# Feed-forward gate and up by seven block products in place of eight, in two passes over the tokens, with the residual added by rows at the end

## The chip, the cores and the metric

The kernel runs on one core of one Trainium2 chip. The metric is device time in microseconds (us), as the median of several executions. TensorE (PE) multiplies and writes to PSUM, eight banks of 512 fp32 numbers per partition; VectorE (DVE), ScalarE (ACT) and GpSimd (POOL) do the rest; SyncE (SP) issues the DMAs here.

## The reference, cut to what matters

One layer of a streaming encoder for 1024 new frames and 32 frames of a running stream, 1056 tokens in all, with 1024 features each. Two kinds of attention come first; the change leaves them alone. What it touches is the tail:

```python
def residual_tail(h, oa, ob, g_out_a, g_out_b, w_out, g_ffn, w_gate, w_up, w_down):
    mixed = jnp.concatenate([rmsnorm(oa, g_out_a), rmsnorm(ob, g_out_b)], axis=-1)
    h = h + mixed @ w_out
    u = rmsnorm(h, g_ffn)
    return h + (jax.nn.silu(u @ w_gate) * (u @ w_up)) @ w_down      # D_FF = 2816
```

and a last `rmsnorm` over each row. All is fp32.

## The kernel before

**Products of fp32 numbers.** Each operand is split into a high and a low part (`hi` is the value rounded to the type fp32r by an ACT copy, `lo` is the rest, a subtraction on DVE), and `product` issues three matmuls: hi with hi, hi with lo, lo with hi (lines 604, 605 and 606). So each matmul "of 128x384" below is one third of a product.

**Stages.** Input projection and both attentions run to about 567 us of the span. Then a stage that this text calls the row stage works tile by tile (nine tiles of 128 tokens, the last of 32): `turn_mixed` transposes attention outputs, `out_product` multiplies by `w_out` (24 matmuls 512 wide), DVE adds the residual `h` in `xb`/`xc`, normalises it to `xn2`, and `turn_residual` transposes both on PE, `xc` (eight transposes, the residual by columns, kept in `y_res`) and `xn2` (eight more, split into `f_hi` and `f_lo`).

**Feed-forward.** The 2816 hidden features are taken 256 at a time (`q`, eleven steps). `gate_up(q)` makes gate and up of two blocks of 128 features over all tokens, in three chunks of 384, 384 and 288 tokens, 8 blocks of input features each; `down(q-1)` follows it on PE. ACT takes silu of the gate in PSUM, DVE multiplies (L1877), ACT and DVE split the hidden values (L1465, L1880), DVE adds the down products to `y_res` in SBUF (L1891, L1894). Weights come by DMA as 512 KB blocks into three `raw` buffers and are split by ACT (L1092) and DVE (L1522), 128x1024 at a time. GpSimd has no instruction in this stage. Each engine's order is written out by hand, and engines meet by semaphores alone: an instruction that waits holds up everything behind it on its engine.

**End.** `last_down` interleaves the last down products with transposes of finished tiles (`turn_out`), ACT squares and takes the root, DVE scales, SP stores.

Of the kernel before, what the change touches and what calls it, by code (L numbers as in the profile page):

```python
# [377 lines left out]
def build(nc, x_p, x_s, ck_fox, cv_fox, cl_fox, ck_swa, cv_swa, rel_bias, g_attn, w_in, b_forget, sinks,  # L380
# [2037 lines left out]
```

## Time and profile before

| | |
|---|---|
| median of three runs | 1425.41 us (1424.62 to 1426.76) |
| the profiled execution, its span | 1425.3 us |
| TensorE busy | 1389.4 us, 97% of the span |
| VectorE, ScalarE, GpSimd busy | 572.3, 484.7 and 213.8 us |
| chain that ended last | PE 91% of the span |
| feed-forward stage, from its first matmul to the last one's start | 635.1 to about 1414.7 us |
| granted clock in the feed-forward stage | 1.00 in the stretches of 100 us from 700 to 1300 us |

The profile is of one execution, whose span differs from the median by 0.1 us. A matmul's duration there holds the fill and the drain of the array, which overlap with its neighbours; what a matmul costs in a stream is the distance from its start to the next one's start, called its pitch here.

### The profile page before, as it was taken

The numbers are of one execution on the slowest core, as the hardware profiler recorded it, in microseconds if no ns is written. First come the engines' busy times: TensorE is split into PE (matmuls) and PEld (weight loads), VectorE is DVE, ScalarE is ACT, GpSimd is POOL, SyncE is SP. The second block draws the span as 40 slices with busy tenths as digits, with TensorE's granted clock in tenths as the row PEclk, the third lists the DMA queues.
The fourth block names the chain that finished last, engine by engine and source line by source line (L and its number), as shares of the span: only waits on it lengthen the run. The fifth ranks groups of instructions, "written<-read, shape, count | busy, mean of one in ns | idle before, by whom it ended". The sixth has DMA issues, their size and how long they took to land.

```text
span 1425.3 us, 22561 instructions
## 1 busy us (share of the span) xinstructions
PE 1389.4 (97%) x9041; PEld 1288.1 (90%) x9041; DVE 572.3 (40%) x1340; ACT 484.7 (34%) x1049; POOL 213.8 (15%) x318
## 2 busy tenths in 40 slices
PE   7999999999999899999999999999999999999998
PEld 5988898788878677889999999999999999999997
DVE  6345634242323433562333434342424252525156
ACT  6356555655554552563212121212121212121103
POOL 3145551644443230000000000000000000000000
PEclk9999999999999899999999999999999999999999
DMA  7621124212120444314202020202020202020003
GB/s 202 115 67 38 32 78 156 81 43 80 51 83 15 150 163 135 109 46 132 61 30 68 22 74 16 74 16 74 16 74 16 75 16 74 16 74 15 30 1 122
DMA packets 110255, 97.64 MB, mean 69 GB/s; under 512 B 15936, under 2 KB 96928, under 8 KB 109640
## 3 DMA queue, kind: packets, MB, share of 16 engines
q1 hardware_dynamic: 110152, 96.20, 23.0%
q8 instruction: 72, 1.18, 0.4%
q14 instruction: 31, 0.25, 0.1%
HBM read 77.07 MB, written 19.21 MB: 68 GB/s over the span
## 4 chain that ended last, share of the span: by engine, by line
PE 91%; DVE 3%; DMA 2%; ACT 2%; issue 2%; POOL 1%; SPq 0%; ACTq 0%; DVEq 0%
PE ps L604 28%; PE ps L605 26%; PE ps L606 26%; PE ps L808 2%; DMA cb<-c_scratch 1%; PE ps L738 1%; PE ps L956 1%; PE ps L820 1%; PE ps L685 1%; PE ps L897 1%; PE ps L776 1%; DVE ps L1650 1%; DMA ob<-o_scratch 1%; ACT sp_x L1279 0%; PE ps L703 0%
## 5 line engine op out<-in xcount | busy, mean ns | idle before, releaser
L1891 DVE TENSOR_TENSOR outs<-outs,ps 128x384 f32<-128x384 f32 (+1 forms) x264 | 134.5, 509 | 108.3 <-PE ps L606 108.0
L1877 DVE TENSOR_TENSOR gu<-ps,sg 128x384 f32<-128x384 f32 (+1 forms) x66 | 34.6, 524 | 237.8 <-PE ps L606 237.8
L2055 POOL TENSOR_TENSOR pl_x<-sp_x,ph_x 128x512 fp32r<-128x512 f32 (+5 forms) x120 | 102.3, 866 | 170.4 <-ACT sp_x L1279 169.0
L1465 ACT ACTIVATE h_hi<-gu 128x384 fp32r<-128x384 f32 (+1 forms) x66 | 32.9, 498 | 222.4 <-DVE gu L1877 222.4
L1278 ACT ACTIVATE ph_x<-ps,negc 128x512 fp32r<-128x512 f32 (+5 forms) x120 | 63.0, 525 | 84.5 <-PE ps L820 84.5
L1459 ACT ACTIVATE sg<-ps 128x384 f32<-128x384 f32 (+1 forms) x66 | 30.5, 465 | 171.7 <-PE ps L606 171.7
L604 PE MATMUL ps<-f_hi,ff0hi 128*128 128x384 f32 (+1 forms) x264 | 85.7, 325 | 0.0
L604 PE MATMUL ps<-f_hi,ff2hi 128*128 128x384 f32 (+1 forms) x264 | 85.6, 324 | 0.0
L604 PE MATMUL ps<-f_hi,ff3hi 128*128 128x384 f32 (+1 forms) x264 | 85.6, 324 | 0.0
L604 PE MATMUL ps<-f_hi,ff1hi 128*128 128x384 f32 (+1 forms) x264 | 85.6, 324 | 0.0
L605 PE MATMUL ps<-f_lo,ff0hi 128*128 128x384 f32 (+1 forms) x264 | 85.3, 323 | 0.0
L605 PE MATMUL ps<-f_lo,ff1hi 128*128 128x384 f32 (+1 forms) x264 | 85.2, 323 | 0.0
L605 PE MATMUL ps<-f_lo,ff2hi 128*128 128x384 f32 (+1 forms) x264 | 85.2, 323 | 0.0
L605 PE MATMUL ps<-f_lo,ff3hi 128*128 128x384 f32 (+1 forms) x264 | 85.2, 323 | 0.0
L606 PE MATMUL ps<-f_hi,ff0lo 128*128 128x384 f32 (+1 forms) x264 | 85.2, 323 | 0.0
L606 PE MATMUL ps<-f_hi,ff1lo 128*128 128x384 f32 (+1 forms) x264 | 85.1, 322 | 0.0
L606 PE MATMUL ps<-f_hi,ff2lo 128*128 128x384 f32 (+1 forms) x264 | 85.1, 322 | 0.0
L606 PE MATMUL ps<-f_hi,ff3lo 128*128 128x384 f32 (+1 forms) x264 | 85.1, 322 | 0.0
L604 PE MATMUL ps<-h_hi,ff4hi 128*128 128x384 f32 (+1 forms) x240 | 82.2, 342 | 0.6 <-DVE outs L1894 0.5
L604 PE MATMUL ps<-h_hi,ff5hi 128*128 128x384 f32 (+1 forms) x240 | 78.2, 326 | 0.0
L1092 ACT ACTIVATE ff4hi<-raw 128x1024 fp32r<-128x1024 f32 x10 | 10.6, 1060 | 197.0 <-PE ps L606 197.0
L605 PE MATMUL ps<-h_lo,ff5hi 128*128 128x384 f32 (+1 forms) x240 | 77.5, 323 | 0.0
(303 smaller groups left out, 3837.5 us busy)
## 6 DMA issues: line engine op xcount, KB each, us to landing
raw<-in_w_gate SPq DMA_DIRECT2D x22, 512.0 KB, 4.5
raw<-in_w_up SPq DMA_DIRECT2D x22, 512.0 KB, 5.0
raw<-in_w_down SPq DMA_DIRECT2D x22, 512.0 KB, 3.9
raw<-in_w_in SPq DMA_DIRECT2D x14, 512.0 KB, 4.0
cb<-c_scratch SPq DMA_DIRECT2D x4, 1312.0 KB, 7.1
xt<-in_x_prompt SPq DMA_DIRECT2D x8, 512.0 KB, 4.7
out<-outb SPq DMA_DIRECT2D x16, 256.0 KB, 2.8
ob<-o_scratch SPq DMA_DIRECT2D x16, 256.0 KB, 3.1
```

Source lines behind the costliest of these rows:

```text
L604: pe.matmul(out, wh, xh, start=start, stop=False)
L605: pe.matmul(out, wh, xl, start=False, stop=False)
L606: return pe.matmul(out, wl, xh, start=False, stop=stop)
L685: mm = pe.transpose(ps[0:m, b, (2 * kv + x) * P:(2 * kv + x + 1) * P], ot_w[kv][:, x * m:(x + 1) * m], ident[:])
L738: pe.matmul(ps[0:rows, 2 + kv, 0:2 * m].rearrange("p (x q) -> p x q", x=2), keys[hs, k0:k0 + rows], queries[half][hs, :, q], start=(part = ...
L808: pe.matmul(ps[0:rows, b + h, 0:n], keys[i % 2][hs, k0:k0 + rows], queries[i % 2][hs, q], start=(part == 0), stop=False)
L1278: act.activation(ph_x[2 * (v % 2) + h][0:rows, 0:n], ps[0:rows, b + h, 0:n], ACT.Exp, bias=decay, scale=-1.0)
L1459: act.activation(sg[c][:, 0:n], bank(c, n), ACT.Silu).then_inc(S["g_sg"], 1)
L1465: act.activation(h_hi[par][:, f, c0:c0 + n], gu[(f + c) % 2][:, 0:n], ACT.Copy).then_inc(S["g_hi"], 1)
L1877: dve.tensor_tensor(gu[(f + c) % 2][:, 0:n], bank(3 + c, n), sg[c][:, 0:n], ALU.mult)\
L1891: add = dve.tensor_tensor(y, y, bank(b, whole * P).rearrange("p (t m) -> p t m", t=whole), ALU.add)
L2055: pool.tensor_tensor(pl_x[at][0:rows, 0:n], sp_x[at][0:rows, 0:n], ph_x[at][0:rows, 0:n].bitcast(F32), ALU.subtract).then_inc(S["x_pl"], 1)
```

## The change

Gate and up together multiply a 2x2 block matrix of weights (gate or up, by the first or the last four blocks of input features) by a 2x2 block matrix of inputs (input features by token half). The new code forms four sums of weight blocks and four of input blocks, makes seven products of blocks 4 x 128 features deep in place of eight, and adds them up: `x1` and `p7` are copied out of PSUM by ACT, five are added by DVE (`add_bank`, L2033), one (`p7`) is added again by GpSimd (`add_fourth`, L2373).

- The tokens are taken in two passes: tokens 0 to 511 in halves of 256, and tokens 512 to 1055 in halves of 272. All weights are loaded and split once in each pass. A set `g` is one block of 128 hidden features in one pass; there are 44 sets (`SETS`), 22 (`NF`) in each pass.
- A set has seven `ffn_product`s of 12 matmuls, 256 or 272 wide, on six PSUM banks; seven weight blocks of 128x512, each split by ACT (L1543) and DVE (L2007) into one of eleven slots; four weight sums on GpSimd (`weight_sums`, 128x512, into the single buffer `sums`). From set 2 on it has four down pieces: 24 matmuls 512 wide in the first pass, 48 of 272 in the second (`down_piece`), added to `y` by DVE (L2073), and one down weight of 128x1024 split (`down_hi`, `down_lo`).
- The seven inputs `fu` have one buffer, so pass 1's are made at sets 20 to 22 (`input_sum` on GpSimd, `input_hi` on ACT, `input_lo` on DVE, 128x1088).
- The residual is no longer transposed. It is stored to DRAM (`x2_scratch`) in the row stage and loaded at the end into `hrow`; `add_row` adds the transposed `y` to it. The rows of pass 0 are finished within sets 24 and 25.

The core of the diff:

```diff
-            def residual_columns(t):
-                columns_lo(t, (6, 7), "c_hi3", 2 * t, f_hi, f_lo, t * P, "c_lo3")
...
+            for g in range(SETS):
+                for i in range(7):
+                    ffn_product(g, i)
+                    if g == 0 and i == 2:
+                        turn_residual(TILES - 1)
+                    if g == NF + 2:
+                        if i < 4:
+                            turn_out(i)
...
+                    elif g >= 2 and 2 <= i < 6:
+                        down_piece(g, i - 2)
...
             def turn_residual(t):
-                pe.wait_ge(S["c_h2"], 2 * (t + 1))
...
-                rows_to_columns(t, xc[t % 2], (4, 5), S["c_t2"])
                 pe.wait_ge(S["c_xn2"], t + 1)
...
+            def add_bank(g, i):
+
+                n, par = HALF_OF[pass_of(g)], g % 2
+                first, x2, x3 = x1[:, 0:n], x23[par][:, 0, 0:n], x23[par][:, 1, 0:n]
+                gate0, gate1 = sg[par][:, 0, 0:n], sg[par][:, 1, 0:n]
+                dst, src = {1: (gate0, first), 2: (x2, first), 4: (x3, x2), 5: (gate1, x3), 6: (x2, x2)}[i]
...
+            def down_group(n, q, j):
...
+                pe.wait_ge(S["f_hl"], 4 * pg + 4)
+                pe.wait_ge(S["dw_lo"], n - 1)
...
+            def weight_sums(g):
+
+                a11, a12, a21 = (fraw[g % 2][:, mat, k:k + 4, :] for mat, k in (A11, A12, (1, 0)))
+                a22 = fraw[g % 2][:, 1, 4:8, :]
+                s1, s2, s3, s4 = (sums[:, SUM_OF[i], :, :] for i in (4, 2, 3, 5))
+                pool.wait_ge(S[f"fw_in{g % 2}"], 32 * (g // 2 + 1))
+                if g >= 1:
+                    pool.wait_ge(S["fw_lo"], 7 * (g - 1) + 5)
+                pool.tensor_tensor(s1, a21, a22, ALU.add).then_inc(S["fw_sum"], 1)
+                pool.wait_ge(S["fw_sum"], 4 * g + 1)
+                pool.tensor_tensor(s2, s1, a11, ALU.subtract).then_inc(S["fw_sum"], 1)
+                pool.tensor_tensor(s3, a11, a21, ALU.subtract).then_inc(S["fw_sum"], 1)
...
+                pool.tensor_tensor(s4, a12, s2, ALU.subtract).then_inc(S["fw_sum"], 1)
...
+            def store_mixed(t):
+
+                m = rows_of(t)
+                sp_.wait_ge(S["c_h2"], 2 * t + 2)
+                sp_.dma_start(x2_dram[t * P:t * P + m, :], xc[t % 2][0:m]).then_inc(S[f"x2_out{t % 2}"], 16)
```

**Where the instructions go on DVE.** Before, in the middle of a feed-forward step, VectorE alternates between gated values (`gu`), their low parts (`h_lo`) and weight splits 128x1024 (`ff0lo` and so on), then adds sixteen down products (`outs`):

```order
L1877 TENSOR_TENSOR gu_190<-ps,sg_189 128x288 [waits g_lo,g_sg,g_mm]
L1880 TENSOR_TENSOR h_lo_125<-gu_190,h_hi_124 128x288 [waits g_hi]
L1522 TENSOR_TENSOR ff0lo<-raw_60,ff0hi 128x1024 [waits cw_hi]
L1522 TENSOR_TENSOR ff1lo<-raw_61,ff1hi 128x1024 [waits cw_hi]
L1522 TENSOR_TENSOR ff2lo<-raw_62,ff2hi 128x1024 [waits cw_hi]
L1877 TENSOR_TENSOR gu_191<-ps,sg_187 128x384 [waits g_lo,g_sg,g_mm]
L1880 TENSOR_TENSOR h_lo_125<-gu_191,h_hi_124 128x384 [waits g_hi]
L1877 TENSOR_TENSOR gu_190<-ps,sg_188 128x384 [waits g_lo,g_sg,g_mm]
L1880 TENSOR_TENSOR h_lo_125<-gu_190,h_hi_124 128x384 [waits g_hi]
L1877 TENSOR_TENSOR gu_191<-ps,sg_189 128x288 [waits g_lo,g_sg,g_mm]
L1880 TENSOR_TENSOR h_lo_125<-gu_191,h_hi_124 128x288 [waits g_hi]
L1891 TENSOR_TENSOR outs<-outs,ps 128x3x128 [waits d_y,d_mm] x16
```

After, these are the first twelve of the nineteen rows of one set in pass 0 on VectorE (`fw` are the weight slots, `sums` and `fraw` what they are split from, `x_0`, `x_1`, `x_199` partial sums, `f_p7`, `f_sg`, `f_add` count GpSimd's, ScalarE's and its own work):

```order
L2033 TENSOR_TENSOR x_1_222<-x_1_222,ps 128x256 [waits f_p7,f_pe]
L2043 TENSOR_TENSOR sg_216<-sg_216,x_1_222 128x256 [waits f_add,f_sg]
L2007 TENSOR_TENSOR fw_196<-sums,fw_196 128x512 [waits fw_hi]
L2007 TENSOR_TENSOR fw_197<-sums,fw_197 128x512 [waits fw_hi]
L2050 TENSOR_TENSOR h_lo_174<-sg_216,h_hi_173 128x256 [waits f_hh]
L2033 TENSOR_TENSOR sg_220<-x_199,ps 128x256 [waits f_x,f_pe]
L2007 TENSOR_TENSOR fw_198<-sums,fw_198 128x512 [waits fw_hi]
L2033 TENSOR_TENSOR x_0_190<-x_199,ps 128x256 [waits f_x,f_pe]
L2073 TENSOR_TENSOR y<-y,ps 128x512 [waits y_add,d_pe]
L2007 TENSOR_TENSOR fw_187<-fraw_175,fw_187 128x512 [waits fw_hi]
L2007 TENSOR_TENSOR fw_188<-fraw_176,fw_188 128x512 [waits fw_hi]
L2073 TENSOR_TENSOR y<-y,ps 128x512 [waits y_add,d_pe]
```

The adds of products now stand among the weight splits, and between the gated value (second row) and its low part (fifth row) stand two splits that wait for ScalarE.

**On ACT.** Over the same stretch ScalarE's row is now (`h_hi` high parts of hidden values, `x_199` a product copied out, `sg` silu):

```order
L1592 ACTIVATE h_hi_214<-sg_220 128x256 [waits f_gu] x2
L1577 ACTIVATE x_199<-ps 128x256 [waits f_add,f_pe]
L1543 ACTIVATE fw_197<-sums 128x512 [waits f_pe,fw_sum]
L1543 ACTIVATE fw_198<-sums 128x512 [waits f_pe,fw_sum]
L1584 ACTIVATE sg_216<-sg_216 128x256 [waits f_add]
L1543 ACTIVATE fw_187<-sums 128x512 [waits f_pe,fw_sum]
```

Silu, and with it the split behind it, now waits for an add on VectorE (`f_add`), and the splits ahead wait behind `h_hi`, which waits for VectorE's gated value (`f_gu`).

**On POOL.** Before, GpSimd's last compute rows are those of the attention:

```order
L2055 TENSOR_TENSOR pl_x_106<-sp_x_161,ph_x_103 32x32 [waits x_e]
L2055 TENSOR_TENSOR pl_x_107<-sp_x_162,ph_x_155 32x32 [waits x_e]
```

After, it has six rows for each set:

```order
L2340 TENSOR_TENSOR sums<-fraw_176 128x512 [waits fw_lo,fw_in0]
L2342 TENSOR_TENSOR sums<-sums,fraw_176 128x512 [waits fw_sum]
L2343 TENSOR_TENSOR sums<-fraw_176 128x512
L2347 TENSOR_TENSOR sums<-fraw_176,sums 128x512 [waits fw_lo,fw_sum]
L2373 TENSOR_TENSOR x_0_190<-x_0_190,p_179 128x256 [waits f_add,f_x] x2
```

All of them are new there, and the first starts when VectorE has finished the second of the two splits after its gated value.

## Rows read from the trace of the kernel before

**Rows 1.** Page, part 1: busy us, share of the span, instructions.

```profile
PE 1389.4 (97%) x9041; PEld 1288.1 (90%) x9041; DVE 572.3 (40%) x1340; ACT 484.7 (34%) x1049; POOL 213.8 (15%) x318
```

**Rows 2.** Windows: stretch, length, busy PE, PEld, DVE, ACT, POOL, clock, DMA share, GB/s.

```profile
800.00:900.00 100.00, 100.00 (x613) 99.15 (x612) 43.34 (x87) 15.48 (x23) 0.00 (x0) 1.00 0.14 41
```

**Rows 3.** Timeline of PE (start us, duration us): streams 384, 288, 256 and 512 wide.

```profile
159.13 0.28 PE L604 MATMUL ps<-ph_w,vs_hi 128*128 128x256 f32 x1
...
159.72 0.28 PE L606 MATMUL ps<-ph_w,vs_lo 128*128 128x256 f32 x1
...
568.75 0.39 PE L604 MATMUL ps<-wo_hi,m_hi 128*128 128x512 f32 x1
...
572.19 0.39 PE L604 MATMUL ps<-wo_hi,m_hi 128*128 128x512 f32 x1
...
899.92 0.34 PE L604 MATMUL ps<-f_hi,ff0hi 128*128 128x384 f32 x1
...
902.03 0.29 PE L604 MATMUL ps<-f_hi,ff0hi 128*128 128x288 f32 x1
...
905.22 0.34 PE L604 MATMUL ps<-f_hi,ff1hi 128*128 128x384 f32 x1
```

**Rows 4.** Timeline of PE: both sets of transposes of tile 7, first feed-forward matmul.

```profile
633.46 1.03 PE L956 MATMUL ps<-ident,xb 128*128 128x128 f32 x8
634.33 1.04 PE L956 MATMUL ps<-ident,raw 128*128 128x128 f32 x8
635.13 0.42 PE L604 MATMUL ps<-f_hi,ff0hi 128*128 128x384 f32 x1
```

**Rows 5.** Groups by form, DVE: count, busy us and mean ns, idle before.

```profile
L1891 DVE TENSOR_TENSOR outs<-outs,ps 128x256 f32<-128x256 f32 x88 | 37.0, 421 | 26.1 <-PE ps L606 25.7
...
L1522 DVE TENSOR_TENSOR ff0lo<-raw,ff0hi 128x1024 fp32r<-128x1024 f32 x12 | 14.7, 1225 | 5.1 <-ACT ff0hi L1092 4.9
...
L1528 DVE TENSOR_TENSOR f_lo<-ps,f_hi 128x512 fp32r<-128x512 f32 x16 | 10.3, 685 | 0.0
```

**Rows 6.** Groups by form, ACT.

```profile
L1263 ACT ACTIVATE ot_w<-ps 128x256 f32<-128x256 f32 x32 | 11.7, 384 | 5.0 <-PE ps L606 5.0
...
L1225 ACT ACTIVATE vw_hi<-outb 128x512 fp32r<-128x512 f32 x8 | 5.1, 632 | 0.3
```

**Rows 7.** Groups by form, POOL.

```profile
L2055 POOL TENSOR_TENSOR pl_x<-sp_x,ph_x 128x512 fp32r<-128x512 f32 x48 | 60.8, 1287 | 61.2 <-ACT sp_x L1279 61.2
L2004 POOL TENSOR_TENSOR pl_w<-sp_w,ph_w 128x256 fp32r<-128x256 f32 x60 | 43.0, 738 | 41.4 <-ACT sp_w L1248 41.3
```

**Rows 8.** Timeline, DVE and POOL, in the first stage.

```profile
16.03 1.28 DVE L1734 SCALAR_TENSOR_TENSOR xn<-xt,small,gains 128x1024 f32<-128x1024 f32 x1
...
17.80 2.41 POOL L1989 TENSOR_TENSOR cw0lo<-raw,cw0hi 128x1024 fp32r<-128x1024 f32 x1 [9.47 <-ACT cw0hi L1092]
...
19.31 1.98 DVE L1734 SCALAR_TENSOR_TENSOR xn<-xt,small,gains 128x1024 f32<-128x1024 f32 x1
```

**Rows 9.** Timeline: two pairs back to back, and a handover from DVE to ACT.

```profile
583.14 1.07 ACT L1413 ACTIVATE outs<-ps 128x512 f32<-128x512 f32 x2
...
913.85 0.56 DVE L1877 TENSOR_TENSOR gu<-ps,sg 128x384 f32<-128x384 f32 x1 [2.45 <-PE ps L606]
...
914.44 0.52 ACT L1465 ACTIVATE h_hi<-gu 128x384 fp32r<-128x384 f32 x1 [3.63 <-DVE gu L1877]
...
941.25 0.46 DVE L1880 TENSOR_TENSOR h_lo<-gu,h_hi 128x288 fp32r<-128x288 f32 x1 [0.51 <-ACT h_hi L1465]
941.62 0.55 DVE L1891 TENSOR_TENSOR outs<-outs,ps 128x384 f32<-128x384 f32 x1
```

**Rows 10.** Timeline of the end: transposes after the last matmul, last store issued.

```profile
1414.69 3.65 PE L1061 MATMUL ps<-ident,outs 128*128 128x128 f32 x32
...
1422.89 0.33 SPq L2362 DMA_DIRECT2D out<-raw  x1
```

**Rows 11.** Page, part 6: DMA issues, KB each, median us from issue to landing.

```profile
raw<-in_w_up SPq DMA_DIRECT2D x22, 512.0 KB, 5.0
```

More of the change, by code:

```diff
@@ new lines, in build @@
+        hrow = (*hrows, *hrows, hrow8)
+        early, end = lay(end, *((f"fw{k}", [P, 2, 4, P], F32R) for k in range(3)))
+        (x23_0,), end = lay(end, ("x23_0", [P, 2, 272], F32))
+        assert end <= reg1 + 8 * D * 4
+        late, end = lay(reg1 + 8 * D * 4, *((f"fw{k}", [P, 2, 4, P], F32R) for k in range(3, SLOTS)))
+        fw = (*early, *late)
+        (x1,), end = lay(end, ("x1", [P, 272], F32))
+        assert end <= reg2
+        u_parts, end = lay(reg2, *((f"fu{k}{n}", [P, 4, 272], F32R) for k in range(7) for n in ("hi", "lo")))
@@ L514, in build @@
+        (x23_1,), end = lay(1184 + P * 4, ("x23_1", [P, 2, 272], F32))
+        h_hi, h_lo, sg, x23 = (h_hi0, h_hi1), (h_lo0, h_lo1), (sg_0, sg_1), (x23_0, x23_1)
         ss_col = small[:, 72:72 + 18]
@@ L1082, in _ @@
+            for k, x in enumerate(GROUPS[LAST0:]):
+                down_group(*x)
+                if k == 10:
+                    turn_out(4)
+                if k == 13:
+                    turn_out(5)
+            for t in range(6, TILES):
                 turn_out(t)
@@ new lines, in copy_out, with silu @@
+            def copy_out(g, x):
+                n = HALF_OF[pass_of(g)]
+                i = 3 * x
+                act.wait_ge(S["f_pe"], 7 * g + i + 1)
+                if g >= 1:
+                    act.wait_ge(*((S["f_add"], 5 * (g - 1) + 2) if x == 0 else (S["f_p7"], 2 * (g - 1) + 2)))
+                act.activation((x1, p7)[x][:, 0:n], bank((7 * g + i) % SPARE, n), ACT.Copy).then_inc(S["f_x"], 1)
+            def silu(g, j):
+                n = HALF_OF[pass_of(g)]
+                act.wait_ge(S["f_add"], 5 * g + (1, 4)[j])
+                part = sg[g % 2][:, j, 0:n]
+                act.activation(part, part, ACT.Silu).then_inc(S["f_sg"], 1)
@@ new lines, in _ @@
+            add_bank(SETS - 1, 6)
+            gated(SETS - 1, 0)
+            hidden_lo(SETS - 1, 0)
+            down_lo(SETS + 1)
+            for k, x in enumerate(GROUPS[LAST0:]):
+                add_group(*x)
+                if k == 12:
+                    add_row(4)
+                if k == 14:
+                    add_row(5)
+            for t in (4, 5):
+                out_roots(t, t + 1)
+                out_row(t)
+            for t in range(6, TILES):
+                add_row(t)
@@ L1951, in _ @@
+            for t in range(6, TILES):
+                out_roots(t, t + 1)
+                out_row(t)
         @block.gpsimd
@@ new lines, in add_fourth @@
+            def add_fourth(g):
+                n, par = HALF_OF[pass_of(g)], g % 2
+                for x in range(2):
+                    pool.wait_ge(S["f_x"], 2 * g + 2)
+                    pool.wait_ge(S["f_add"], 5 * g + 3 + x)
+                    part = x23[par][:, x, 0:n]
+                    pool.tensor_tensor(part, part, p7[:, 0:n], ALU.add).then_inc(S["f_p7"], 1)
+            pool.wait_ge(S["g_pe"], NT)
+            pool.wait_ge(S["ev_act"], ALL_ACT)
+            pool.wait_ge(S["ev_dve"], ALL_DVE)
@@ L2365, in _ @@
+            sp_.wait_ge(S["fw_sum"], 4 * (SETS - 1))
+            sp_.wait_ge(S["fw_lo"], 7 * (SETS - 1))
+            load_result_row(8)
+            for t in range(4, TILES):
+                store_result(t)
             sp_.wait_ge(S["st_y0"], 16 * 3)
```

779 lines of the change are left out of this document (479 added, 300 removed).

## The prediction

> **What bounds the kernel now.** I read the page first: TensorE is busy 97% of the span [rows 1]. Then the windows: in the feed-forward stage PE is busy all the time at clock 1.00, while DVE has 43 us of work in 100, ACT 15, POOL none [rows 2]. So that stage lasts as long as its stream of matmuls, and the price of one is its pitch. Twelve starts 384 wide go from 899.92 to 902.03, 0.1755 us each; 24 of 288 from there to 905.22, 0.1329. Five of 256 take 0.59 us, 0.118 each, and 15 of 512 take 3.44 us, 0.2293 [rows 3]. For 272 I take 0.1255, between 256 and 288.
>
> **What PE saves.** Before: gate and up are 22 x 2 x 8 x 3 = 1056 matmuls for each chunk, down 528, and 1584 x (2 x 0.1755 + 0.1329) = 766 us. After: 22 x 84 = 1848 matmuls of 256 (218.1) and as many of 272 (231.9); down 528 of 512 (121.1) and 1056 of 272 (132.5), in all 704 us. That is 62 less. The residual's transposes go too: 0.87 us a tile, the start distance of the two blocks of eight [rows 4], 7.0 for the eight tiles before the first feed-forward matmul.
>
> The Trainium skill (TensorE: Matmul & The Clock Gate, Back-to-back issue gap) gives N/2.4 + 2.5 ns; by it the sum would be 709 us before and 652 after, 57 less. The trace's pitches are 8% longer, and I go by them.
>
> Per set PE then needs 84 x 0.118 + 24 x 0.2293 = 15.4 us in pass 0 and 132 x 0.1255 = 16.6 in pass 1. The question is whether the other engines keep this pace.
>
> **What a set costs DVE, ACT and POOL.** Durations: DVE 0.42 for 256, 0.69 for 512, 1.22 for 1024 [rows 5]; ACT 0.38 for 256 from PSUM, 0.63 for 512 from SBUF, and 0.42 (estimate between these) for 256 from SBUF [rows 6]; POOL 1.29 for 512, 0.74 for 256 [rows 7]. Independent neighbours on DVE start 0.09 before the end (941.25 + 0.46, next at 941.62); two ACT copies of 0.584 take 1.07 together, so 0.10 there; a handover between engines takes 0.03 [rows 9]. DVE's nineteen instructions of a set in pass 0 (7 splits and 4 down adds of 512, one split of 1024, nothing else above 256: 5 adds, 2 gated, 2 low parts) come to 11 x 0.60 + 1.13 + 9 x 0.33 = 10.7 us: below 15.4. But two things stand between them.
>
> First, **exchanges with ACT**: DVE's first splits wait for ACT's, which stand behind `h_hi` and so behind DVE's own gated value; later splits stand behind silu, which waits for DVE's add.
>
> Second, **the port to SBUF**: one DVE instruction with both inputs in SBUF, normally 1.28 us, took 1.98 when a POOL tensor_tensor was running at its start. POOL ended at 20.21, DVE 1.08 later, about the time to stream 1024 elements [rows 8]. So it stood still until POOL was done; for 512 elements I take half, 0.54 after POOL's end, for 1024 1.08. POOL is new in this stage, and all splits, gated values and low parts on DVE have both inputs in SBUF.
>
> The Trainium skill (SBUF — State Buffer, Who interferes with whom) says this: such a DVE instruction and a GpSimd one that reads SBUF exclude each other, and whoever starts first holds the shared port for its whole instruction. The trace agrees.
>
> **A walk through one set**, t = 0 at its first row on DVE, with PE ahead. Add 0 to 0.42; gated 0.45 to 0.87. ACT: `h_hi` 0.90 to 1.32, copy out 1.22 to 1.60, two splits to 2.13 and 2.66. DVE: two splits 2.16 to 2.85 and 2.76 to 3.45, low part to 3.78, add to 4.11. ACT: silu 4.14 to 4.56, split 4.46 to 5.09. DVE split 5.12 to 5.81. POOL's first sum starts when the low part frees the port, 3.78 to 5.07; the second waits for that split, 5.81 to 7.10. DVE: add and down add to 6.74; next split held by POOL, ends 7.64. Third sum to 8.93, split ends 9.47, fourth sum to 10.76; down add to 10.07; the split of 1024, held, ends at 10.76 + 1.08 = 11.84. From there add, split, down add, add: 1.86, to 13.70. Silu 13.73 to 14.15, ACT split to 14.68, DVE split 14.71 to 15.40, gated to 15.73, `h_hi` 15.76 to 16.18, low part to 16.63; the next set starts at 16.54. The sum: 10.7 of work, 3.3 waiting for ACT, 2.5 for the port.
>
> This loop does not contain PE. Two things can only lengthen it: at 5.1 split and second sum ask together (the other outcome adds about 0.5), and POOL may keep the port through queued sums (then 18.0). I take 16.9 for pass 0. Pass 1 has eight down adds at 0.35 for four at 0.60 and nine instructions 0.02 longer: + 0.55, 17.45. Both are above PE's 15.4 and 16.6; PE then waits, for a hidden low part before a down piece (`f_hl`) or for a bank. Were the sums on POOL free of the port, the loop would be 14.1, hidden under PE.
>
> **Edges.** (a) Row stage: DVE has input splits of 128x1024 from tile 6 on, seven of 1.2, for the `f_lo` of 1.3 a tile that go: + 3. The residual's store and the reload behind it have two tiles' time. First product at 635.1 - 7.0 + 3 = 631. (b) Sets 0 and 1: DVE first finishes the last tile (7.6), then splits twelve weights in set 0, with ACT's and POOL's share 16, then 14.5 for set 1, which lacks 2.4 of down adds: 38, where PE needs 20. (c) Sets 20 to 22: 51 + seven input splits 8.4 + four sums of 2.5 on POOL, of which about 6 falls on DVE: 66. (d) Sets 23 to 25: 52 + four row adds of 1.2 and four row scalings of 1.2, and 3 for PE's transposes in turn: 65. (e) Sets 42 and 43 split almost nothing more: PE's 16.6. (f) End: 2 for the last low part, 16 groups of six matmuls (0.75) with two `turn_out`s and the row adds between, 15, then row adds, squares, scalings for five tiles. Before, 10.6 us lay from the last matmul to the end [rows 10]; the new end adds row adds (1.2 each) ahead of the squares: 14. In all 31.
>
> Weight traffic doubles, from 66 blocks of 512 KB (22 of each matrix) to 132, three per set; against the 5.0 us from issue to landing [rows 11] a set of over 15 us leaves it hidden.
>
> **Sum**: 631 + 38 + 18 x 16.9 (304) + 66 + 65 + 16 x 17.45 (279) + 33 + 31 = 1447. The profiled execution of before took 1425.3 and the median 1425.4, so 1447 stands against both. Rounded, as the terms allow no more: **1445 us**, 1.4% slower.
>
> **Rivals.**
> 1. *PE sets the pace* (0.30), the other side. Mechanism: DVE and POOL share the port at less cost, or ACT runs far enough ahead that its exchanges vanish. For it: DVE's work alone is 10.7 of 15.4. Against it: the 1.98 us of rows 8. Time: 629 + 33 + 18 x 15.4 + 56 + 55 + 18 x 16.6 + 29 = 1378; with half the edges' stalls not recovered, 1390. It decides from 0.5 us less per set on: a loop under 16.4 and 16.95 gives below 1425.
> 2. *POOL keeps the port through its four sums* (0.12): 18.0 and 18.55 per set, 34 x 1.1 = 37 more, 1482.
> 3. *Transfers come late* (0.06): two raw buffers, one for down weights, and a gate load that stands behind a down load on SP. If three blocks together took over 8 us, each us more delays POOL's sums by one: + 1 on 34 sets, 1479.
>
> The forecast itself has 0.52, with 1428 to 1472 as its own range. Cases of both signs hold much of the chance: the range goes from rival 1, 1388, to between forecast and rival 2, 1474. Bounds of the unknown cost of the port: nothing (14.1, PE's pace, 1390) and POOL first throughout (1482). A measurement of this kernel tells some 0.2% (3 us) from no change. Faster 0.32 (rival 1, little of the forecast), within it 0.05, slower 0.63.
>
> **What would show it.** In the profile after: matmul pitches 0.118, 0.125 and 0.23, PE work 62 us less; PE idle 1 to 2 us per set, put down to DVE; DVE splits 128x512 with a mean well over 0.69 (about 0.9), single ones up to 1.9, while adds from PSUM stay at 0.42; sets 16.5 to 17.5 us apart. I would be wrong if the splits kept 0.69 next to POOL, if PE is busy throughout sets 3 to 19 (rival 1), or if the splits wait over 3 us at once (rival 2).

## The result, and the profile after

Median of 4 runs after the change: **1473.88 us** (1471.06 to 1477.22); before, in the same series, 1426.09 (1424.62 to 1427.72). Ratio 1.0339, 95% interval 1.0321 to 1.0358: the change makes the kernel 3.4% slower. The forecast was 1445, 1.4% slower: the direction is right, the size is not (48 us more than before, forecast 20). The measured time lies at the upper end of the stated range of 1388 to 1474, and beyond the forecast's own 1428 to 1472. The profiled execution has a span of 1471.1 us.

The page of the kernel after, part 1 (for [rows 1]) and, of part 5, the new groups of VectorE and GpSimd (busy us, mean ns, idle before):

```profile
PE 1354.3 (92%) x9497; PEld 1220.8 (83%) x9497; DVE 914.1 (62%) x1804; ACT 674.9 (46%) x1462; POOL 586.3 (40%) x590
...
L2007 DVE TENSOR_TENSOR fw<-sums,fw 128x512 fp32r<-128x512 f32 x176 | 163.2, 949 | 139.5 <-ACT fw L1543 139.5
...
L2007 DVE TENSOR_TENSOR fw<-fraw,fw 128x512 fp32r<-128x512 f32 x132 | 140.5, 1083 | 12.1 <-ACT fw L1543 11.9
...
L2343 POOL TENSOR_TENSOR sums<-fraw 128x512 f32<-128x512 f32 x44 | 77.8, 1769 | 0.0
```

A split of 512 that took 0.69 us in [rows 5] now takes 0.95 or 1.08 in the mean, a sum of 1.29 on GpSimd [rows 7] takes 1.77, and VectorE waits 139.5 us for ScalarE's high parts.

The same kernel's windows (columns as in [rows 2]): sets 0 and 1; the steady part of pass 0; sets 20 to 22; sets 23 to 25; the rest of pass 1:

```profile
631.00:684.00 53.00, 36.92 (x256) 34.64 (x254) 41.60 (x56) 25.88 (x53) 29.22 (x20) 0.84 0.30 83
684.00:993.00 309.00, 289.42 (x1943) 267.15 (x1942) 241.28 (x379) 126.53 (x252) 144.70 (x110) 0.97 0.34 93
993.00:1062.00 69.00, 54.31 (x332) 49.53 (x331) 53.87 (x71) 28.57 (x50) 30.38 (x19) 0.88 0.33 99
1062.00:1133.00 71.00, 58.02 (x407) 55.92 (x406) 51.24 (x82) 27.93 (x53) 26.92 (x21) 0.90 0.24 68
1133.00:1417.00 284.00, 272.44 (x2118) 267.99 (x2117) 221.36 (x401) 113.38 (x224) 122.89 (x92) 1.00 0.35 101
```

Before, TensorE was busy in all of the stretch of [rows 2]. Now it idles about 1 us a set in the steady parts (1.1 in pass 0, 0.7 in pass 1) and much more at the start and at the change of passes.

**One set, seen on VectorE and GpSimd** (timeline of both engines in the kernel after; start us, us):

```profile
744.43 1.35 POOL L2340 TENSOR_TENSOR sums<-fraw 128x512 f32<-128x512 f32 x1 [5.66 <-DMA fraw<-in_w_up]
...
745.86 1.29 POOL L2342 TENSOR_TENSOR sums<-sums,fraw 128x512 f32<-128x512 f32 x1
745.96 1.75 DVE L2007 TENSOR_TENSOR fw<-sums,fw 128x512 fp32r<-128x512 f32 x1 [1.00 <-ACT fw L1543]
747.09 1.79 POOL L2343 TENSOR_TENSOR sums<-fraw 128x512 f32<-128x512 f32 x1
...
747.62 0.41 DVE L2033 TENSOR_TENSOR x<-x,ps 128x256 f32<-128x256 f32 x1
...
748.55 0.88 DVE L2007 TENSOR_TENSOR fw<-fraw,fw 128x512 fp32r<-128x512 f32 x1
748.83 1.76 POOL L2347 TENSOR_TENSOR sums<-fraw,sums 128x512 f32<-128x512 f32 x1
750.06 1.08 DVE L2007 TENSOR_TENSOR fw<-fraw,fw 128x512 fp32r<-128x512 f32 x1 [0.64 <-ACT fw L1543]
```

GpSimd's second sum ends at 747.15; the split that asked at 745.96 ends at 747.71, 0.56 later. The third sum ends at 748.88, the next split at 749.43, 0.55 later; the fourth at 750.59, the split at 751.14, 0.55 later. The prediction had 0.54. And the third and fourth sums start before the split ahead of them has ended and last 1.8 where 1.29 is usual: GpSimd is held by VectorE in its turn. The add of 0.41, with one input in PSUM, runs in the middle of the third sum at its usual length [rows 5].

**The sum against the trace.** VectorE's split of a down block (L2058) stands once in each set. The first and last start in four stretches of the kernel after (one line's instructions: count, ns min, median and max, first and last start):

```profile
L2058 DVE TENSOR_TENSOR dw<-draw,dw x19: 1206/1212/1726, 683.7 to 992.6; 128x1024 fp32r<-128x1024 f32 x19
...
L2058 DVE TENSOR_TENSOR dw<-draw,dw x4: 1210/1468/1724, 992.6 to 1061.7; 128x1024 fp32r<-128x1024 f32 x4
...
L2058 DVE TENSOR_TENSOR dw<-draw,dw x4: 1209/1220/1724, 1061.7 to 1133.2; 128x1024 fp32r<-128x1024 f32 x4
...
L2058 DVE TENSOR_TENSOR dw<-draw,dw x17: 1210/1211/1626, 1133.2 to 1416.6; 128x1024 fp32r<-128x1024 f32 x17
```

In the prediction's walk this split begins 10 us into a set, so its terms read 679 for the mark of set 2 (631 + 38 + 10) and 54 from the mark of set 42 to the end (33 + 31 - 10). In the table, each run's marks are read in the same way (the expectations of e8 and e16 give 74.6 and 66.2 us for stretches between other marks; here these are 69.1 and 71.5). e1, e3, e4, e7, e8, e15 and e16 are the experiments below; "PE only" is rival 1 (629 + 33 + 10, 18 x 15.4, 56, 55, 16 x 16.6, 52).

| us | forecast | PE only | after | e1 | e3 | e4 | e7 | e8 | e16 | e15 |
|---|---|---|---|---|---|---|---|---|---|---|
| mark of set 2 | 679 | 672 | 683.7 | 674.1 | 674.7 | 678.6 | 671.1 | 683.3 | 683.8 | 680.2 |
| sets 2 to 19 | 304 | 277 | 308.9 | 286.3 | 286.2 | 280.2 | 280.0 | 305.9 | 305.1 | 280.4 |
| sets 20 to 22 | 66 | 56 | 69.1 | 64.0 | 63.7 | 65.4 | 61.4 | 54.8 | 68.7 | 62.7 |
| sets 23 to 25 | 65 | 55 | 71.5 | 66.2 | 66.4 | 63.3 | 62.8 | 71.5 | 65.7 | 63.3 |
| sets 26 to 41 | 279 | 266 | 283.4 | 267.3 | 267.5 | 268.1 | 265.8 | 283.5 | 283.2 | 265.6 |
| to the end | 54 | 52 | 54.5 | 56.0 | 55.9 | 55.9 | 54.5 | 54.5 | 53.4 | 54.6 |
| span | 1447 | 1378 | 1471.1 | 1413.9 | 1414.4 | 1411.5 | 1395.5 | 1453.5 | 1459.8 | 1406.6 |

### The profile page after: what moved, and what is told of

It is laid out like the page before. It is cut to its first block, busy times and chain, and to the rows that moved or that the text cites. A ratio compares the mean times of both kernels' runs of the same rounds, so it can differ in the third digit from the quotient of the medians.

```text
span 1471.1 us, 26068 instructions
## 1 busy us (share of the span) xinstructions
PE 1354.3 (92%) x9497; PEld 1220.8 (83%) x9497; DVE 914.1 (62%) x1804; ACT 674.9 (46%) x1462; POOL 586.3 (40%) x590
## 4 chain that ended last, share of the span: by engine, by line
PE 49%; DVE 23%; issue 13%; ACT 8%; DMA 4%; SPq 1%; POOL 1%; DVEq 0%; ACTq 0%; POOLq 0%
PE ps L702 14%; PE ps L704 13%; PE ps L703 13%; DVE fw L2007 6%; ACT fw L1543 4%; DVE y L2073 3%; PE ps L906 2%; DVE x L2033 2%; DVE sg L2043 2%; DVE h_lo L2050 2%; DVE dw L2058 2%; DVE sg L2033 2%; DMA fraw<-in_w_up 1%; PE ps L836 1%; DMA cb<-c_scratch 1%
## 5 line engine op out<-in xcount | busy, mean ns | idle before, releaser
L2007 DVE TENSOR_TENSOR fw<-sums,fw 128x512 fp32r<-128x512 f32 x176 | 163.2, 949 | 139.5 <-ACT fw L1543 139.5
L702 PE MATMUL ps<-h_hi,dw 128*128 128x272 f32 (+1 forms) x528 | 181.1, 343 | 64.3 <-DVE h_lo L2050 45.5
L2340 POOL TENSOR_TENSOR sums<-fraw 128x512 f32<-128x512 f32 x44 | 62.8, 1426 | 295.7 <-DVE fw L2007 208.8
L704 PE MATMUL ps<-h_hi,dw 128*128 128x272 f32 (+1 forms) x528 | 175.9, 333 | 0.0
L703 PE MATMUL ps<-h_lo,dw 128*128 128x272 f32 (+1 forms) x528 | 175.0, 331 | 0.0
L702 PEld LDWEIGHTS ps<-h_hi,dw 128*128 128x128 f32 x528 | 102.1, 193 | 77.5 <-DVE h_lo L2050 48.4
L2007 DVE TENSOR_TENSOR fw<-fraw,fw 128x512 fp32r<-128x512 f32 x132 | 140.5, 1083 | 12.1 <-ACT fw L1543 11.9
L2373 POOL TENSOR_TENSOR x<-x,p 128x256 f32<-128x256 f32 (+1 forms) x88 | 79.7, 908 | 171.1 <-DVE x L2033 134.9
L1543 ACT ACTIVATE fw<-fraw 128x512 fp32r<-128x512 f32 x132 | 82.3, 627 | 122.2 <-PE ps L704 117.5
L2073 DVE TENSOR_TENSOR y<-y,ps 128x272 f32<-128x272 f32 (+1 forms) x240 | 117.4, 511 | 10.7 <-PE ps L704 10.6
L704 PEld LDWEIGHTS ps<-h_hi,dw 128*128 128x128 f32 x528 | 102.2, 194 | 8.2
L703 PEld LDWEIGHTS ps<-h_lo,dw 128*128 128x128 f32 x528 | 102.9, 195 | 4.3
L1543 ACT ACTIVATE fw<-sums 128x512 fp32r<-128x512 f32 x176 | 104.3, 618 | 1.1 <-PE ps L704 0.9
L2343 POOL TENSOR_TENSOR sums<-fraw 128x512 f32<-128x512 f32 x44 | 77.8, 1769 | 0.0
```

The costliest lines, as they stand in the source:

```text
L702: pe.matmul(out, wh, xh, start=start, stop=False)
L703: pe.matmul(out, wh, xl, start=False, stop=False)
L704: return pe.matmul(out, wl, xh, start=False, stop=stop)
L1543: act.activation(fw[e % SLOTS][:, 0, :, :], weight_block(g, i), ACT.Copy).then_inc(S["fw_hi"], 1)
L2007: dve.tensor_tensor(lo, weight_block(g, i), hi.bitcast(F32), ALU.subtract).then_inc(S["fw_lo"], 1)
L2073: dve.tensor_tensor(dst, dst, bank(6 + at % 2, width), ALU.add).then_inc(S["y_add"], 1)
```

## The experiments

Except for e14 and e15 each time is that of one execution, and executions of one kernel lie up to 6 us apart (1471.06 to 1477.22 above). Beside these single executions the kernel before took 1423.8 to 1426.0. The stretches of the table say more than the totals: e14 is the same kernel as e4, and its trace reads 680.0, 280.1, 65.3, 63.3, 268.0 and 54.5, so the four in the middle repeat within 0.1 and the first and last within 1.4. Where TensorE has pauses, sets 2 to 19 repeat less well, within 3 to 4 (308.9 in the kernel after, 305.1 in e16, whose edit does not touch them).

### The port: e1, e2, e3

e1; e2 has `0:2, 0:128` in place of `0:1, 0:32`, and the other three sums are cut likewise:

```
-                return sums[:, SUM_OF[i], :, :]
+                return fraw[g % 2][:, i % 2, 0:4, :]
...
-                pool.tensor_tensor(s1, a21, a22, ALU.add).then_inc(S["fw_sum"], 1)
+                pool.tensor_tensor(s1[:, 0:1, 0:32], a21[:, 0:1, 0:32], a22[:, 0:1, 0:32], ALU.add).then_inc(S["fw_sum"], 1)
```

> GpSimd's four sums of a set write 32 of 512 columns; the splits of the summed weights read the raw gate and up blocks instead, at the same places and with the same semaphores (this leaves out Strassen's weight sums). GpSimd then reads SBUF for about 0.1 us four times a set in place of 1.3 to 1.8. Theory A (the loop of VectorE, ScalarE and GpSimd sets the pace; port and exchanges add up): without the port's 2.5 us the loop falls to about 14.1 to 14.5, TensorE takes over at 15.4 and 16.6, splits 128x512 return to 0.69, 1410 to 1425 us. Rival B (the exchanges with ScalarE alone, the port costs nothing): sets stay at 17.0 and 17.8, 1465 to 1471. Rival C (TensorE or its clock sets the pace): no change, 1471.

Measured: 1415.87 us.

> As the run with 32 columns, but the four sums write 256 of 512 columns (about 0.7 us each). Theory A: the port costs about half, the loop is about 15.5, near TensorE's pace, so nearly all of the gain is there already: 1415 to 1435. Rival B: 1465 to 1471. If the loss is proportional to GpSimd's time and the loop is bound throughout: half way between the run with 32 columns and 1471.

Measured: 1423.0 us.

e3, with the first of those two edits and, for each of the four sums:

```
-                pool.tensor_tensor(s1, a21, a22, ALU.add).then_inc(S["fw_sum"], 1)
+                pool.wait_ge(S["fw_sum"], 4 * g + 0)
+                pool.memset(sums[:, 0:3, :, :], 0.0).then_inc(S["fw_sum"], 1)
```

> GpSimd works as long as before (four instructions of about 1.3 us a set, at the same places in its queue and behind the same semaphores), but each is a memset of 1536 columns that reads nothing from SBUF; the splits read the raw blocks (this leaves out the weight sums). Theory A (what costs is the port that both read SBUF through): splits at 0.69 and the time of the run with 32 columns, 1410 to 1425. Rival D (not the port but the length of GpSimd's chain, whose late sums hold the splits): stays near 1471. If a memset holds the port as well: splits above 0.69 as now, and 1460 or more.

Measured: 1416.34 us. e3, groups of 700 to 900 us, the splits and one of the four memsets:

```profile
L2007 DVE TENSOR_TENSOR fw<-fraw,fw 128x512 fp32r<-128x512 f32 x90 | 60.6, 690 | 43.8 <-ACT fw L1543 43.8
...
L2343 POOL MEMSET sums<- 128x1536 f32 x13 | 18.0, 1386 | 0.7
```

and e3's window of 700 to 800:

```profile
700.00:800.00 100.00, 99.13 (x685) 91.53 (x683) 72.99 (x135) 45.40 (x90) 49.38 (x40) 1.00 0.35 96
```

GpSimd is busy 49 us in 100, more than the 45 of the kernel after, and the splits are back at 0.690. So not GpSimd's time nor its place in the chain costs the 57 us, but that its instructions read SBUF while VectorE's read two inputs there. The Trainium skill (SBUF — State Buffer, Who interferes with whom) has this rule too: such a VectorE instruction contends with one of GpSimd that reads SBUF, not with one that only writes it; e3 agrees. Rivals B, C and D of the expectations fall. The waits for ScalarE are still there (43.8 us here, 42.2 in the same 200 us of the kernel after) and cost nothing now. In e2, sums of half the width bring back 50 of the 57 us, and all of what sets 2 to 19 and 26 to 41 have to give (286.2 and 267.5 us, as in e1): the loop need only fall to TensorE's pace, and below it a shorter one gains nothing, which is why the gain is not in proportion.

### The exchanges with ScalarE: e4, e12, e13

e4; e12 is its first moved pair alone, e13 the other two (`silu` for 0 and 1):

```
-                if g >= 1:
-                    hidden_hi(g - 1, 0)
...
                 weights_hi(g, 0)
-                silu(g, 0)
+                if g >= 1:
+                    hidden_hi(g - 1, 0)
                 weights_hi(g, 1)
+                silu(g, 0)
...
-                silu(g, 1)
                 weights_hi(g, 4)
+                silu(g, 1)
```

> Only ScalarE's order changes, the computation is whole: the high parts of the weights stand ahead of the hidden high part and of both silus, so VectorE's splits find them done. Theory A: the 3.3 us of waiting for ScalarE go from the loop (17.0 to about 14), TensorE takes over: sets 15.5 and 16.8, 1400 to 1425. Port alone (rival E, the exchanges are hidden anyway): 1460 to 1471. If the port's share grows because VectorE now meets GpSimd more often: 1430 to 1450.

Measured: 1413.4 us. e4's windows:

```profile
700.00:800.00 100.00, 100.00 (x703) 93.30 (x702) 88.30 (x137) 45.93 (x91) 53.56 (x39) 1.00 0.38 103
...
1200.00:1300.00 100.00, 100.00 (x796) 100.00 (x795) 82.94 (x152) 43.05 (x85) 49.96 (x36) 1.00 0.36 96
```

and its splits of 700 to 900 us:

```profile
L2008 DVE TENSOR_TENSOR fw<-sums,fw 128x512 fp32r<-128x512 f32 x52 | 45.3, 892 | 11.6 <-ACT fw L1543 11.2
L2008 DVE TENSOR_TENSOR fw<-fraw,fw 128x512 fp32r<-128x512 f32 x39 | 42.2, 1088 | 2.9 <-ACT fw L1543 2.7
```

VectorE's waits for ScalarE fall from 42 to 14 us in these 200, the splits stay as long as in the kernel after (0.89 and 1.09), VectorE is busy 88 of 100, and TensorE is busy throughout. The port costs as much as before and nothing waits for it.

> The changed kernel, whole, with one edit of ScalarE's order: the high parts of the two weights that VectorE splits first in a set stand ahead of the hidden high part. In the prediction's walk VectorE waits 1.3 us there (0.87 to 2.16), and 0.3 at the second split; with PE's pace at 15.4 and 16.6 and sets of 17.0 and 17.7, about half of the way: sets of 15.6 to 16.0 and 16.7 to 17.0, 1430 to 1445. If the waits only move to the next exchange: 1460 or more.

Measured: 1434.27 us; steady sets 15.5 in pass 0 and 17.45 in pass 1, the second above its range.

> The other two edits of ScalarE's order alone: the high part of the weight behind each silu stands ahead of it. In the walk VectorE waits 1.0 us at the first silu (4.11 to 5.12) and 1.1 at the second (13.57 to 14.71), 2.1 together: sets of 15.4 to 15.6 and 16.6 to 16.8 in the steady stretches, 1418 to 1432. If these waits are hidden by the port's stalls: 1455 or more.

Measured: 1429.93 us; steady sets 15.8 and 16.8 (e4: 15.5 and 16.8). In pass 0 either edit brings the loop to or near TensorE's pace, in pass 1 only the silus' does; that the two gains are so unequal there was not in the walk, and its reason stays open.

### Both away: e7

The edits of e1 and e4 together.

> Both causes taken away: ScalarE's order as in the run of 1413.4, and GpSimd's sums 32 columns wide with the raw blocks split (leaves out the weight sums). If port and exchanges are two parts of one loop, either alone already brings it under TensorE's pace, and together they give little more, only at the change of passes: 1398 to 1410, sets of 15.4 and 16.6. If the two gains add (58 each), far less: 1355.

Measured: 1397.35 us, just below the range. e7's windows of sets 2 to 19 and 26 to 41:

```profile
671.00:951.00 280.00, 279.08 (x1946) 259.86 (x1946) 217.95 (x379) 126.60 (x252) 62.43 (x109) 1.00 0.38 102
...
1075.00:1341.00 266.00, 266.00 (x2115) 266.00 (x2114) 201.63 (x401) 113.46 (x224) 52.70 (x92) 1.00 0.38 108
```

Gains of 57 (e1) and 60 (e4) do not add; together they are 76, the rest of it mostly at the start and in sets 20 to 22. This is the kernel in which TensorE sets the steady pace, 15.5 and 16.6 us a set, and it takes 1397, not rival 1's 1378: the steady sets match its terms and sets 20 to 25 exceed them by 13.

### Transfers: e5, e6

The three blocks stood behind `load_down_raw`, at NF, NF + 4 and NF + 7:

```
                 load_ffn_raw(k + 2)
+                if k == NF + 1:
+                    sp_.wait_ge(S["u_lo"], 14)
+                    for t in range(4):
+                        sp_.wait_ge(S[f"x2_out{t % 2}"], 16 * (5 - t % 2))
+                        load_result_row(t)
+                if k == NF + 5:
+                    for t in range(4):
+                        store_result(t)
+                if k == NF + 8:
+                    for t in range(4, 8):
+                        load_result_row(t)
                 if k >= 1:
                     load_down_raw(k + 2)
```

> Only SyncE's order changes: the loads of result rows 0 to 3 and 4 to 7 and the stores of rows 0 to 3 stand behind the gate and up loads of the next set in place of ahead of them. In the trace after the change two sets of pass 1 take 22.3 and 22.5 us with their sums waiting for the up block, followed by 14.5 and 14.0. If late transfers matter (rival 3 of the prediction), 8 to 12 us go, 1461; by the loop theory the short sets behind already give most of it back, and 2 to 4 us go: 1467 to 1470.

Measured: 1467.26 us. By the marks sets 23 to 25 fall from 71.5 to 68.0 and sets 26 to 41 from 283.4 to 282.1; the other three stretches ahead of them differ by -1.4, -0.5 and +0.9. So late transfers are worth some 5 us (3.5 + 1.3), by rows queued ahead of a set's gate and up blocks. In the kernel after, two first sums of sets 26 to 40 waited for such an up block, in e5 none did. The weights' own traffic is less well hidden than the prediction had it. Among the first sums of sets 2 to 19 of the kernel after, four of 18 waited for the up block last, as here:

```profile
881.16 1.31 POOL L2340 TENSOR_TENSOR sums<-fraw 128x512 f32<-128x512 f32 x1 [6.23 <-DMA fraw<-in_w_up]
```

but the usual wait, for VectorE's split, is 5.66, so this one, the longest of the four, cost 0.6 us at most. Rival 3's mechanism is there in these sets, but hardly its price.

> The run with ScalarE's order changed (1413.4) and SyncE's order of the run before this one together. With TensorE the bound, a wait of the sums for the up block matters only where it reaches TensorE (about 1.5 us at each of two places): 1408 to 1412. If transfers are what is left between this kernel and TensorE's pace, 1400 or less.

Measured: 1414.67 us, no gain over e4's 1413.4 (a miss): sets 26 to 41 fall from 268.1 to 265.9, but sets 23 to 25 take 0.9 more and set 2's mark comes 3.4 later, in a part that the edit doesn't touch.

### The change of passes and the residual's rows: e8, e16

e8, in which VectorE's low part is cut as ScalarE's high part is, then e16:

```
-                act.activation(fu[i][0][:, :, 0:n], staged(p, *U_FROM[i]), ACT.Copy).then_inc(S["u_hi"], 1)
+                act.activation(fu[i][0][:, :, 240 * p:n], staged(p, *U_FROM[i])[:, :, 240 * p:n], ACT.Copy).then_inc(S["u_hi"], 1)
...
-                b11, b12, b21, b22 = (staged(p, k, j) for k in range(2) for j in range(2))
+                b11, b12, b21, b22 = (staged(p, k, j)[:, :, 240 * p:] for k in range(2) for j in range(2))
```

```
-                dve.tensor_tensor(hrow[t][0:m], hrow[t][0:m], ps[0:m, b:b + 2, :].rearrange("p b n -> p (b n)"), ALU.add)\
+                dve.tensor_tensor(hrow[t][0:m, 0:32], hrow[t][0:m, 0:32], ps[0:m, b, 0:32], ALU.add)\
```

> The changed kernel with the input sums and splits of pass 1 cut to columns 240 to 271 (leaves out the rest of pass 1's operands, TensorE multiplies what pass 0 left there); all else as it is. It prices term (c): VectorE loses seven splits of 1.3 us, GpSimd three of its four sums of 2.5 us. If these hold sets 20 to 22, they fall from 74.6 us to 53 to 57, and the whole to 1450 to 1455; if the passes' change costs by the operands that TensorE must release first, it stays above 65 and the whole above 1462.

Measured: 1455.48 us, at the range's upper end. Sets 20 to 22 fall by 14.3, to 54.8, and the interval ahead of them, in which the first input sum of pass 1 now runs, by 2.7 (19.7 to 17.0). The input work was priced at 14.4 in term (c) (8.4 + 6); it costs 17.0, or a little more, as 32 of 272 columns were left.

> The changed kernel with the nine additions of the residual rows at the end cut to 32 of 1024 columns (leaves out the rest of the residual and of the result); loads, squares, scalings and stores stay. It prices the row adds of terms (d) and (f): 1.1 us less for each of nine, four in the set of pass 1 where TensorE's transposes wait for them in turn, three to four on the path at the end. By the prediction's terms 4 to 5 us less in sets 23 to 25 (66.2 to about 61.5) and 3 to 4 at the end: 1463 to 1467. If they are hidden: 1471 to 1474.

Measured: 1461.93 us, a little below the range. Sets 23 to 25 fall by 5.8, the end by 1.1 (3 to 4 were expected there). Of the rest of the 11.3 us of the spans, 3.8 lie in sets 2 to 19, which this edit does not touch.

### The sums on VectorE: e9, e10

Both take `weight_sums` of sets 2 to 43 from GpSimd and put its four instructions on VectorE: the first behind `down_lo`, the second behind the next `add_bank`, the third behind `add_bank(g, 5)`, the fourth at the set's end. e10 has e4's order of ScalarE as well.

```
                 down_lo(g + 1)
+                weight_sum(g + 2, 0)
                 add_bank(g, 4)
+                weight_sum(g + 2, 1)
```

> The changed kernel, whole, with the weight sums of sets 2 to 43 on VectorE in place of GpSimd (four instructions of 0.69, 0.60 from start to start, so 2.4 us more work a set); GpSimd keeps only the two short sums of 256 or 272 columns. By the loop theory the port's 2.5 us are exchanged for 2.4 us of work in the same loop: sets stay at 16.8 to 17.3 and 17.5 to 18, 1463 to 1475. If the port cost more than the theory says, faster than 1455; if VectorE's work was hidden and only GpSimd's late sums counted, 1420.

Measured: 1480.92 us; steady sets 17.4 and 17.8.

> The same sums on VectorE together with ScalarE's order changed (the run of 1413.4). VectorE has 10.7 + 2.4 = 13.1 us of work a set and waits for neither port nor ScalarE: below TensorE's 15.4, so steady sets as in the run of 1413.4; at the change of passes, where VectorE is the bound, the port's stalls of up to 3.3 us on single splits are gone but 2.4 us a set are added: 1405 to 1416.

Measured: 1429.62 us; steady sets 15.7 and 17.3.

Both miss their ranges on the slow side. The port's 2.5 us a set are gone, and 2.4 us of instructions in VectorE's queue cost as much or more. In e9 most sets of pass 0 take 16.9 as in the kernel after; the mean is raised by three of 18.3 to 20.0, in which the granted clock is 0.83 to 0.91. e10 shows it best, at 1.00: VectorE has 88 us of work in 100 in pass 1, as in e4's pass 0, yet its sets take 17.3 where TensorE needs 16.6. That the sums stand ahead of the adds for which the silus wait is the likely reason; a run with other places was not made.

### Squares and scalings spread: e11

e4 with e5's order (its stores and second loads two sets later still), and `out_squares(t)` and `out_row(t)` of rows 0 to 3 one by one in sets 25 to 27:

```
-                if g == NF + 3:
-                    out_roots(0, 4)
-                    for t in range(4):
-                        out_row(t)
...
+                if g in (NF + 4, NF + 5):
+                    out_row(2 * (g - NF - 4))
```

> ScalarE's order and SyncE's order changed as before, and the four squares, four row scalings of the finished rows 0 to 3 spread one by one over the sets behind, in place of four in a row. In the trace of the run of 1414.7 the sets of the scalings took 19.7 and 19.3 in place of 16.6, with TensorE waiting 3.1 twice for a hidden low part: about 6 us less, 1405 to 1410. If the waits come from something else, 1413.

Measured: 1413.06 us, no difference from e4, where 1405 to 1410 was expected. The stalls move from one set to the next (sets 26 to 41: 267.3 against 268.1) and are not less.

### A version faster than both: e14, e15

e15 is e4 and e5 with GpSimd's input sums 1 to 3 of pass 1 put on VectorE, behind the splits that they wait for:

```
                 if g == NF - 1:
                     input_lo(1, 0)
+                    input_sum(1)
```

> The kernel with ScalarE's order changed, whole, the same file as in the run of 1413.4, timed. By its one look: 0.8% faster than the kernel before, 0.991 to 0.993 of it.

Measured: 1415.04 us in the median of five, ratio to the kernel before 0.9931 (0.9917 to 0.9944).

> ScalarE's order, result rows behind the next set's loads, and the three input sums of pass 1 that lie in the change of passes on VectorE in place of GpSimd. In the trace of the run of 1413.4 these three sums of 2.5 us hold VectorE's splits for 2.3, 2.0 and 2.25 us; on VectorE each costs 1.28: about 2.7 us less, and 1 for the rows: 1409 to 1412, 0.989 to 0.991 of the kernel before.

Measured: 1408.05 us in the median of four, just below its range, ratio 0.9878 (0.9862 to 0.9894), against 1424.79 for the kernel before beside both. With ScalarE's queue in another order alone, the seven products are 0.7% faster than the eight; with e15's two further edits, 1.2%. Both gains are small, but neither interval holds 1.

## Why the prediction was right in direction and wrong in size

- **PE's saving**: right. Without port and exchanges a set takes 15.5 and 16.6 (e7), forecast 15.4 and 16.6, and TensorE is busy 1327.5 us in e7, 61.9 less than before (forecast 62). In the kernel after, the same 9497 matmuls keep it busy 1354.3 us, only 35.1 less, as many run at the lower clock (below).
- **The port**: right. a split of VectorE's that meets a sum ends 0.55 us after it (0.54 forecast), adds from PSUM keep their 0.41, and the memsets of e3 show that it is the reading of SBUF that costs. Rival 2 is refuted by the timeline above: between queued sums a waiting split gets its turn.
- **The loop**: right as a mechanism. e3 and e4 each remove one of its parts, each frees TensorE, and together they gain little more than alone. The walk's 16.9 and 17.45 are 16.99 (sets 3 to 18) and 17.71 (sets 26 to 41). The walk said that without the port the loop would hide under PE; the runs show the same of the exchanges. Port and exchanges were not 2.5 and 3.3 us each to be paid, but a loop 1.5 us above TensorE's pace in pass 0 and 1.1 in pass 1; either one, taken away, pays for both.
- **(a)**: right, the first feed-forward product starts at 631.3.
- **The 24 us between the sum, 1447, and the span** are spread over the terms, by the marks. **(b)** + 4.7. **Sets 2 to 19** + 4.9: 2.8 in the last interval, 19.7 long, as the first input sum of pass 1 already falls on a split in it, which (c) had counted later, and 2.1 in the other seventeen. In these VectorE waited for TensorE three times, 1.6 us in all, after falls of its clock (last section), where the walk said: "This loop does not contain PE." The split that the input sum held:

```profile
976.79 2.54 POOL L2358 TENSOR_TENSOR st_b<-st_b 128x1088 f32<-128x1088 f32 x1
...
976.96 2.93 DVE L2007 TENSOR_TENSOR fw<-sums,fw 128x512 fp32r<-128x512 f32 x1 [1.00 <-ACT fw L1543]
```

- **(c)** + 3.1, or 5.9 with that last interval: its input work is 17.0 in place of 14.4 (e8), its base of 51 is 54.8. **(d)** + 6.5: the row adds cost 5.8 in place of 4.8 (e16), and 3.5 come from rows loaded ahead of a set's gate and up blocks (e5), which rival 3 had at a chance of 0.06 and for another reason, the weights' own traffic. **(e) and (f)** + 0.5. **Sets 26 to 41** + 4.4: 16 x 0.26, the extra 0.55 of pass 1 in the walk is 0.72. Here too VectorE waits for TensorE, 14 times and 4.9 us in all, at the clock's upper level; one of them (timeline of the kernel after):

```profile
1262.33 0.44 DVE L2033 TENSOR_TENSOR sg<-x,ps 128x272 f32<-128x272 f32 x1 [0.30 <-PE ps L704]
```

The step that failed is the sizing of the edges, (b), (c) and (d): each was summed from the instructions that were added, at their own durations, as though at the start and at the change of passes the loop lost nothing beyond them. They and the last interval before set 20 came out 17.1 us too short (4.7 + 3.1 + 6.5 + 2.8) of the 24. All six stretches came out longer, none shorter. e7 shows the same of rival 1: steady terms exact, sets 20 to 25 too short by 13. How much of (b) and of the bases of (c) and (d) is the lower clock (below) and how much waiting was not separated, so the cause of those parts stays open.

The steady sets account for 6.5 us more. There it is "This loop does not contain PE" that does not hold: of VectorE's waits in it, 1.6 and 4.9 us are for TensorE. No run separates what these waits add.

That 1473.88 lies inside the range, by 0.1 us, is luck: the range's upper end was taken from rival 2, in which GpSimd keeps the port, and that is not what happened.

Three slips of the prediction changed nothing of this: its list of VectorE's "nineteen instructions" of a set adds up to 21, and its 10.7 us count all 21; rival 1's "from 0.5 us less per set on" gives 1447 - 34 x 0.5 = 1430, and 1425 needs 0.65; and the range's lower end, 1388, lies above rival 1's own 1378.

## What to carry to other kernels

Work moved to GpSimd is not free for VectorE when both read SBUF: count the rest of GpSimd's instruction for each VectorE instruction with two SBUF inputs that meets it, and let GpSimd keep what reads nothing. When a loop of helper engines is a little above the bound, look first at the order within a queue: here three swaps on ScalarE were worth 60 us and left the port's cost in place, hidden. The errors of many small terms, each estimated by adding instructions, did not cancel here: price the transitions (first sets, change of passes) from the waits of a stretch and not from work alone.
